# One pair of sample-state products moved from the mixer to the joint with the second FFN, in bank 0

## What is computed

```
h = rms_norm(x, g_pre)
f = (silu(h @ w_gate) * (h @ w_up)) @ w_down
x = x + 0.5 * rms_norm(f, g_post)
...
S_new = exp(b_last)[..., None] * S + einsum('bhsk,bhsv->bhkv', kc * exp(b_last - b), vc)
...
x = x + rms_norm(concat(groups) @ w_out, g_post)
```

## Time and profile before

| What | Value |
|---|---|
| runs, device time | median 1414.17 us of 3 (1412.22 to 1415.55) |
| profiled execution, its own time | 1413.74 us |
| its span, first to last instruction | 1412.1 us |
| PE busy | 1391.5 us, 99% of the span |
| DVE busy | 896.1 us, 63% |
| ACT busy | 733.7 us, 52% |
| POOL busy | 182.6 us, 13% |
| mean granted TensorE clock | 0.998 of full |

### The profile page before, as it was taken

How to read it: one execution, slowest core, us unless ns; L and a number is a source line. 1 busy time by engine, 2 the same in 40 slices (tenths; PEclk the granted TensorE clock), 3 DMA queues, 4 the chain that set the end, 5 groups by cost and what they waited for, 6 DMA issues and landing times.

```text
span 1412.1 us, 26875 instructions
## 1 busy us (share of the span) xinstructions
PE 1391.5 (99%) x10531; PEld 1319.6 (93%) x10531; DVE 896.1 (63%) x1493; ACT 733.7 (52%) x1195; POOL 182.6 (13%) x333
## 2 busy tenths in 40 slices
PE   7999999999999999999999999999999999999998
PEld 6999999988878999999999999999888799999998
DVE  5666534669995766654467665346899848765542
ACT  4544443489766554443355444345887665444441
POOL 1020000323262020000000000011433510000000
PEclk9999999999999999999999999999999999999999
DMA  9475555567798495545545554564768995555441
GB/s 242 145 210 150 143 146 155 155 197 228 215 313 251 126 271 149 149 141 151 157 131 150 151 148 139 152 178 141 241 206 240 295 254 156 150 150 149 145 142 51
DMA packets 391554, 249.41 MB, mean 177 GB/s; under 512 B 16513, under 2 KB 379638, under 8 KB 391428
## 3 DMA queue, kind: packets, MB, share of 16 engines
q1 hardware_dynamic: 375602, 204.94, 51.1%
q0 software_dynamic: 15520, 42.62, 9.5%
q10 hardware_dynamic: 306, 0.13, 0.0%
HBM read 242.10 MB, written 5.53 MB: 175 GB/s over the span
## 4 chain that ended last, share of the span: by engine, by line
PE 94%; ACT 2%; DVE 1%; DMA 1%; issue 1%; SPq 0%; DVEq 0%; ACTq 0%
PE bank L592 24%; PE bank L593 24%; PE bank L594 24%; PE bank L849 3%; PE bank L960 2%; PE bank L864 2%; PE bank L628 2%; PE bank L632 2%; PE bank L629 2%; PE bank L1037 1%; PE bank L814 1%; DMA raw<-in_ffn_w_gate 1%; PE bank L941 1%; PE bank L1077 1%; PE bank L1079 1%; PE bank L1078 1%
## 5 line engine op out<-in xcount | busy, mean ns | idle before, releaser
L1575 DVE TENSOR_TENSOR w_l<-raw,w_h 128x1024 fp32r<-128x1024 f32 (+1 forms) x332 | 395.1, 1196 | 294.8 <-ACT w_h L1210 294.7
L592 PE MATMUL bank<-hh,w_h 128*128 128x320 f32 x1632 | 512.6, 314 | 0.0
L594 PE MATMUL bank<-hh,w_l 128*128 128x320 f32 x1632 | 504.3, 309 | 0.0
L593 PE MATMUL bank<-hl,w_h 128*128 128x320 f32 x1632 | 504.2, 309 | 0.0
L1210 ACT ACTIVATE w_h<-raw 128x1024 fp32r<-128x1024 f32 (+1 forms) x332 | 332.1, 1030 | 142.1 <-DMA raw<-in_ffn_w_down 103.2
L592 PEld LDWEIGHTS bank<-hh,w_h 128*128 128x128 f32 x1632 | 306.4, 188 | 10.5 <-issue 8.6
L593 PEld LDWEIGHTS bank<-hl,w_h 128*128 128x128 f32 x1632 | 306.5, 188 | 0.6
L594 PEld LDWEIGHTS bank<-hh,w_l 128*128 128x128 f32 x1632 | 306.3, 188 | 0.0
L592 PE MATMUL bank<-guh,w_h 128*128 128x320 f32 x704 | 217.7, 309 | 0.0
L594 PE MATMUL bank<-guh,w_l 128*128 128x320 f32 x704 | 217.3, 309 | 0.0
L593 PE MATMUL bank<-gul,w_h 128*128 128x320 f32 x704 | 217.3, 309 | 0.0
(11 more groups left out here) (286 smaller groups left out, 1595.6 us busy)
## 6 DMA issues: line engine op xcount, KB each, us to landing
raw<-in_ffn_w_gate SPq DMA_DIRECT2D x88, 512.0 KB, 4.0
raw<-in_ffn_w_up SPq DMA_DIRECT2D x88, 512.0 KB, 3.9
raw<-in_ffn_w_down SPq DMA_DIRECT2D x64, 448.0 KB, 3.8
raw<-in_w_in SPq DMA_DIRECT2D x44, 512.0 KB, 3.9
raw<-in_ffn_w_down SPq DMA_DIRECT2D x32, 512.0 KB, 4.1
kpg<-in_cache_sb_k SPq DMA_DIRECT2D x112, 128.0 KB, 3.3
kpg<-in_cache_sb_k POOLq DMA_DIRECT2D x112, 128.0 KB, 2.6
raw<-in_w_out SPq DMA_DIRECT2D x16, 512.0 KB, 6.9
```

Source lines behind the costliest of these rows:

```text
L592: pe.matmul(out, w_h[:, slot, k, :], rhs_h[:, k0 + k, :], start=first, stop=False)
L593: pe.matmul(out, w_h[:, slot, k, :], rhs_l[:, k0 + k, :], start=False, stop=False)
L594: last = pe.matmul(out, w_l[:, slot, k, :], rhs_h[:, k0 + k, :], start=False, stop=end)
L1575: V(dve.tensor_tensor(w_l[:, slot, 0:n, :], raw[:, slot, 0:n, :], w_h[:, slot, 0:n, :].bitcast(F32), ALU.subtract), sm["w_lo"])
```

## The change

Pair 1's products leave the mixer and are made at the joint, as the last of three pairs there, in bank 0 in place of bank 3. Since ACT reads bank 0 for the norm's root, PE waits for `r_ready` before them. DVE's updates of pair 1 move from the mixer into `settle_in`, behind those of pairs 2 and 3 and ahead of the last two weight splits. `STATE_ORDER` gives the count of `st_prod` that a pair's updates wait for. The mixer's output projection waits for 4 updates in place of 8. In the second FFN, the two waits for 12 and 16 updates become one for 16, ahead of the first unit behind the entry, which writes bank 0.

```diff
@@ ffn, on PE @@
-                        if k2 % 2 and i == t == 1:
+                        if k2 % 2 and i == 1 and t == 0:
                             pe.wait_ge(sm["st_done"], 16 * (k2 // 2) + 16)
                         unit(U0 + 4 * i + 2 * t, ffn_bank(i, 2 * t)[:, 0:T], hh, hl)
                         if i == 1 and t == 0:
...
                             x_mean(M, bank[3])
-                            if k2 % 2:
-                                pe.wait_ge(sm["st_done"], 16 * (k2 // 2) + 12)
@@ mixer, on PE @@
                 state_products(0)
                 pe.wait_ge(*at("conv_d", 2))
-                state_products(1)
...
-                pe.wait_ge(*at("st_done", 8))
+                pe.wait_ge(*at("st_done", 4))
@@ joint, on PE @@
                 state_products(2)
                 state_products(3)
+                pe.wait_ge(sm["r_ready"], 2 * M1 + 2)
+                state_products(1)
                 ffn(2 * l + 1, 3 * l + 2, U + U_FFN2)
@@ new_states, settle_in and mixer, on DVE @@
-                    dve.wait_ge(sm["st_prod"], l * per["st_prod"] + pair + 1)
+                    dve.wait_ge(sm["st_prod"], l * per["st_prod"] + STATE_ORDER.index(pair) + 1)
...
-                        new_states(M // 3, (2, 3))
+                        new_states(M // 3, (2, 3, 1))
...
-                new_states(l, (0, 1))
+                new_states(l, (0,))
...
-S_BANK = (2, 3, 1, 2)
+S_BANK = (2, 0, 1, 2)
+STATE_ORDER = (0, 2, 3, 1)
```

## The result

The changed kernel took 1419.8 us (median of 7 runs, 1418.02 to 1423.1), the kernel before 1413.61 us beside it (7 runs, 1410.08 to 1415.55). The ratio is 1.0053, 95% interval 1.0043 to 1.0062: slower by half a per cent. The prediction was 1420.9 us, range 1416.6 to 1423.2, slower with a chance of 0.90.

A forecast was written before the change was run, and what follows sets the result against it. PE was taken to bound the kernel, busy for 99% of the span. The terms -1.45 + 0 + 5.8 + 2.8 = +7.15 us, on the profiled 1413.74, gave 1420.9 us, range 1416.6 to 1423.2.

The forecast's parts named there:

- Part 1: Mixer: pair 1's products leave PE, -0.95 us in layer 0 and -0.5 in layer 1; bounds 0 and -2.25.
- Part 2: Joint of mixer and second FFN: 0.945 us of products fill 0.93 us of idle time, cost 0 to 0.1.
- Part 3: First unit behind the entry: PE waits for DVE's twelve updates, 2.2 and 3.6 us, +5.8; bounds 5.6 and 6.0.
- Part 4: Behind both new stalls TensorE's clock falls to half, 1.4 us each, +2.8 us; bounds 0 and 3.0.
- one clock fall, or none: Stalls behind the entry stand, clock falls once or never: 1419.5 or 1418.1 us; chances 0.18 and 0.14.
- DMA keeps the mixer's gain: Mixer's loads and pages land where they did, no gain there, rest as forecast: 1422.3 us; chance 0.10.
- Does not open a stall: At the entry, usually slower than profiled, the change only swaps places: +2.5 us, 1416.2; chance 0.05.
- faster: DVE's updates end before the entry does; the mixer's gain and layer 0's clock fall are saved: 1410.9 us; chance 0.03.

The follow-up runs named there:

- experiment 1: Changed kernel with DVE's pair 1 updates taken first and PE's one wait for sixteen split into 8, 12 and 16: 1410.63 us, ratio 0.9989.
- experiment 2: Changed kernel with the twelve updates at their place but pair 1's first, and PE's waits split into 8, 12, 16: 1414.31 us, ratio 1.0011.
- experiment 3: Changed kernel with six matmuls of constants into unused bank 3 ahead of PE's wait: 1418.0 us, ratio 1.0036.
- experiment 5: Kernel before with only one of pair 1's eight products in each layer: 1411.18 us, ratio 0.9989.
- experiment 6: Experiment 1 with w_out's last four loads released by the first half of values(7), not by the end of values(6): 1415.32 us, ratio 1.0014.
- experiment 4: Kernel before, products unmoved, with only PE's wait for sixteen updates moved ahead of the first unit behind the entry: 1420.05 us, ratio 1.0049.
- experiment 8: Kernel before with only experiment 1's order on DVE, products, banks and waits as before: 1412.21 us, ratio 1.0.
- experiment 7: Experiment 1 with half a head of the projection on PE ahead of values(7): 1412.44 us, ratio 0.9992.

## Why the prediction was right, and where not

**Part 1, the mixer: right in mechanism, too large in layer 1.** The forecast was -0.95 in layer 0 and -0.5 in layer 1; the ledger has -1.21 and +0.65. Layer 0 kept all of it and 0.3 us of the projection's wait with it, as its upper bound allowed. Layer 1 went beyond its bound of 0: I counted only the 0.16 us that the last page had waited before, and took it that the pages come at fixed times. They do not. SP began its issues for vpg1b 3.75 us behind the first state product, as before, but the eight took 5.38 us in place of 4.88 (one of them 1.28 us), and the last page landed later. A page of vpg1a was late too. By starts, the two halves of values that waited came 0.63 and 0.85 us later than before, 1.5 us in all, while the products had given 0.87: values(5) begins 1.02 us behind the first of them in place of 1.89. So 0.945 was a little too much as well. That is one execution. Over the six kernels with less work ahead of the pages (the changed one, experiments 1, 2, 3, 5 and 6) PE or its weight loads waited for a page in 5 of 12 mixers, over the three with all of it (before, experiments 4 and 8) in 1 of 6.

The forecast's 0.5 for layer 1 was too much beyond this profile too. It rested on the 7.4 us page being the odd one. In the ten traces the last of SP's eight pages for values(7) in layer 1 took 4.8 to 7.6 us, and over 7.2 in four of them. With pair 1 moved and nothing else changed in the mixer, layer 1's mixer gained 0.47, 0.20 and 0.30 us in experiments 1, 2 and 3 and lost 0.65 here, against the 38.95 of before.

**Part 2, the joint: right.** 3.63 us from the mean of squares to the entry, before and after, in both layers. The 0.945 us of products costs nothing there. That only fills PE's idle time; it was never the gain.

**Part 3, the wait: right in mechanism and size.** DVE's twelve updates took 3.19 us (forecast 3.20), PE went on 0.05 us behind them (0.06), and stood for 3.33 and 3.34 us. Entry and wait grew by 2.11 and 3.50 us; with the late first matmul, 0.1 us each by experiments 2 and 3, that is 5.8 us, the forecast's 5.8. Experiment 4 shows that this needs no moved product, experiment 1 that DVE's order removes it. In words of the step: the end of the stall was set by DVE's chain from the norm's root, so layer 0 lost less only because its entry had run slow before.

**Part 4, the clock: right, and now shown.** 2.8 us forecast, 2.81 measured (experiment 3). The rule of the Trainium skill, page TensorE: Matmul & The Clock Gate, section HAM oscillation, that a waiting array comes back at half its clock, is borne out for the gaps of 3.3 us, 2 of 2 times in the trace. The array need not wait for it, though: the seven falls in the mixers came with PE busy. The joint's fall did go, and saved nothing, as said. That both falls were in the profile of after is in part luck. By the estimate of experiment 3, two falls of 1.64 us take 0.0023 off the mean granted clock, which leaves 0.998 at most. The fastest of the seven runs, 1418.02 us, had 0.999, so at most one fall in it: the rival "one clock fall, or none" holds in that run. Experiment 4, with 2.3 us, fell once in two.

**The sum.** By the ledger +8.06 us against +7.15, so the sum was 0.9 us too small, all of it part 1. The measured median lies 1.1 us below the predicted 1420.9 all the same: the scatter of the runs, by first loads (2 us between the two profiles) and by falls of the clock elsewhere, is larger than either, and the ratio's interval reaches from 6.1 to 8.8 us. So that the median hit this closely is in part luck. Of the rivals, "DMA keeps the mixer's gain" (1422.3) has the right mechanism for layer 1 alone. "Does not open a stall" and "faster" both fell at the row on st; the 1410.9 us that "faster" gave for a DVE done in time is what experiment 1 measured, 1410.63.

**What stays open.** Why the last of the eight pages on SP's queue sometimes takes 7.2 to 7.6 us where the median is 4.3 to 4.4. Experiment 6 excludes the last four loads of w_out as the only cause. Whether it is POOL's pages of the same moments, or which rows the pages lie in, was not tried. Open too is why the clock falls behind one gap and not behind another of the same length, and why it fell behind 7 of the 40 rows of 8-column matmuls.

**The best version** is experiment 1: 0.9989 of the kernel before, with an interval (0.9977 to 1.0) that reaches no difference, and about 9 us below the changed one.

## What to carry to other kernels

- When work is moved into an engine's idle time, look at who consumes its result and which wait that moves forward: the products cost nothing at the joint, and the wait for their updates cost 5.8 us and the clock 2.8 more. Put the consumer first in the other engine's order, and wait before each use for just what it needs.
- An idle gap of an otherwise full PE is worth more than its length: here 3.3 us of idle time cost 4.8 (3.33 + 0.1 + 1.4) where the clock fell behind it, and 1.3 us cost 1.4 where it didn't.
- Build the sum against a ledger of stages, not against whole executions; 2 us of first loads, or one fall of the clock elsewhere (1.6 us), can hide or feign a gain of this size.

## What the runs showed of the hardware

- How often TensorE's granted clock fell behind an idle gap in a dense stream of matmuls: 3.3 us, 2 of 2; 2.2 to 2.3 us, 2 of 3 (experiments 4 and 6); 1.3 us, 0 of 2; 0.93 us at the joint behind state products, 2 of 8 (before and experiments 4, 5 and 8). The clock fell behind one and not behind the other of two gaps of the same length in one execution, so length alone doesn't decide.
- It also fell with no idle time: behind 7 of 40 rows of 32 matmuls of 8 columns (experiments 1, 2, 3, 4, 6 and 7), at 1.6 us each.
- A fall cost 1.3 to 1.5 us in the first unit (4.91 - 3.63 and 5.15 - 3.62), and 1.4 us at a joint (15.71 and 15.73 against 14.33 us).
- The first matmul behind a wait hands on 0.1 us later than the others: a unit of 3.52 us becomes 3.62.
- With the DMA engines busy for 0.94 to 0.97 of 1124 to 1138 us (after and before), the last of SP's eight pages for values(7) of layer 1 took 4.8 to 7.6 us over the ten traces. The median page of vpg1b took 4.3 (after) and 4.4 (experiment 6). One of SP's eight issues took 1.28 us after and 1.41 in experiment 8, where 0.33 is usual.
